# Router logits from raw residual rows, the norm factor on the logits, experts chosen for three tiles then two, rows scaled on GpSimd

## Chip, cores and metric

The kernel runs on 1 core of one Trainium2 chip. The metric is the device time of one execution in microseconds (us). Before the change it is 1668.53 us, the median of 3 runs (1665.18 to 1670.41).

## What is computed

One inference step of a one-layer encoder, over 512 prompt rows and 128 decode rows of width 1024, all in float32. The change is confined to the mixture of experts at the end and to the residual sum ahead of it:

```python
x1 = x + merged @ w_out
y  = x1 + hmoe(x1, ffn_norm_g, ...)

def rmsnorm(x, g):
    return x * lax.rsqrt(jnp.mean(x * x, axis=-1, keepdims=True) + EPS) * g

def mix(hb):                                   # hb: 128 rows of rmsnorm(x1, ffn_norm_g)
    g_logit = hb @ w_group_router + b_group_router            # 4 groups
    g_idx, g_w = argmax(g_logit), softmax(g_logit)[g_idx]
    e_logit = (hb @ w_expert_router + b_expert_router).reshape(-1, 4, 8)[g_idx]
    top_p, top_i = top_k(softmax(e_logit), 2)                 # 2 of the group's 8 experts
    top_p = top_p / sum(top_p)
    combine = one_hot(g_idx * 8 + top_i) * (g_w * top_p)
    hid = silu(hb @ w_exp_gate[e]) * (hb @ w_exp_up[e])       # per expert e, width 256
    return sum over e of (hid * combine[e]) @ w_exp_down[e]
```

## The kernel before

There are five tiles of 128 rows (NT = 5): tiles 0 to 3 are the prompt, tile 4 the decode rows. D_MODEL is cut into KD = 8 pieces of 128. Every engine has its own instruction list, written out by hand in build(), and semaphores hold them together. A float32 matmul of the program shows as two records in the trace.

The end of the program, where the change lies, runs as follows.

1. **Output projection** (TensorE, L1147 to L1160). For each half c of the columns, and in it for each tile t, eight matmuls `merged x w_out` fill a PSUM bank (L1157). The bank of item n is ps[4 + n % 2], so item n waits until VectorE has summed item n-2. VectorE adds each bank to the residual x1 (L2056); the x1 rows were loaded by GpSimd's queue shortly before.
2. **Norm**. After the second half of a tile ScalarE squares and sums x1 (L1612, `h2_squared`), VectorE makes the factor in twelve tiny instructions (`rstd`, L1676 to L1682) and scales the rows into h2 with one instruction (L2015, in `ffn_normed`): x1 times the factor times the gain g_ffn. It reads x1 and the gain with a step of 8 elements, since the expert weights are laid out "(p k)".
3. **Router logits** (TensorE). `h2_transposes(t)` (L1136) makes eight transposes of h2, ScalarE copies them to h2T (L1618), and `router_logits(t)` (L1143) multiplies with the 36 router columns w_rt. Tile t-1 is transposed behind item (t, 1); logits of t-2 stand in the middle of item (t, 1). So tiles 3 and 4 have their transposes or logits behind the last item.
4. **Choice of experts** (VectorE, `route(t0, t1)`, L2018 to L2050). Once for tiles 0 to 3 and once for tile 4, some twenty linked small instructions each. They start only when the last tile is scaled. Their logits lie in ps[2] (tiles 0 to 3) and ps[3].
5. **Ranks** (TensorE, L1170 for tiles 0 to 3; L1174 to L1177 for tile 4 and the totals): how many tokens before this one chose the same expert. `marked_at` (L2080 to L2082, VectorE) turns the ranks into one-hot rows, `pairs_at` (L1183, TensorE) multiplies these with the pair numbers, and `tables` (L2090 to L2093, VectorE) makes the list of rows for each expert.
6. **Experts**. GpSimd gathers the rows of a pair of experts from h2_rows in HBM (L2358, `take_rows`), where it has written the scaled tiles (L2352). TensorE transposes them (L1209), then gate and up (L1223), then down (L1246). Each of 32 experts has 3 MB of weights, in five slots. SyncE's queue refills a slot when the matmuls that read it are done (`gu_full`, `dn_full`): experts 0 to 4 are loaded ahead, expert 5 only after the first gate and up.

```python
for e in range(NES, NE):
    n = (e - NES) // 2
    sp.wait_ge(gu_full, n + 1)
    load_gate(e)
    load_up(e)
    sp.wait_ge(dn_full, 2 * (n + 1))
    load_down(e)
```

The router's weights, biases and the gain are loaded by SyncE's queue (L499 to L503) just before the projection; VectorE waits for all five (rtw_in) before the first bank sum.

## Time and profile before

| | us |
|---|---|
| runs | 1668.53, 1670.41, 1665.18 |
| the profiled execution | 1668.23 |
| its span, first to last instruction | 1666.5 |
| TensorE busy in the span | 1525.9 (92%) |
| VectorE busy | 540.0 (32%) |
| ScalarE busy | 294.9 (18%) |
| GpSimd busy | 112.9 (7%) |
| mean granted TensorE clock | 0.959 |

The profile is one execution. Times in its rows count from the first instruction. Engines are PE (TensorE matmuls), PEld (TensorE weight loads), DVE (VectorE), ACT (ScalarE), POOL (GpSimd) and SP (SyncE); a q behind a name is the engine's sequencer, which issues DMAs. Busy shares are averages over stages with different limits: they don't tell what one stage waits for.

### The profile page before, as it was taken

Reading aid. Unit: us, or ns where it says so; the run is one execution under the profiler, and the core shown is the slowest. Engines: PE = TensorE matmul, PEld = TensorE weight load, DVE = VectorE, ACT = ScalarE, POOL = GpSimd, SP = SyncE. Lnnn points to the kernel's source line nnn. Section 1 sums busy time; section 2 is a strip of 40 time slices with the busy share of each in tenths; the row PEclk is TensorE's granted clock in tenths of the full one; section 3 lists DMA queues with packets and bytes.
Section 4 is the critical chain, followed back from the end, with each engine's and each line's share of the span. In section 5 each row is a group of like instructions: output and inputs, shape, how many; then the busy total and the mean of one; then the engine's idle time right before and its main releaser. Section 6 shows DMA issues by size and latency. Waiting matters only on the chain.

```text
span 1666.5 us, 16956 instructions
## 1 busy us (share of the span) xinstructions
PE 1525.9 (92%) x6626; PEld 848.2 (51%) x6626; DVE 540.0 (32%) x1513; ACT 294.9 (18%) x682; POOL 112.9 (7%) x172
## 2 busy tenths in 40 slices
PE   5999999998799999988999999899999997888882
PEld 3554655445455544455555544566554464444441
DVE  2205498206400031443001144234464263101013
ACT  3214211213200011134110011234300011101010
POOL 6000000112000000000000100100000001101100
PEclk9999999899899999999999999999999978989896
DMA  7331120111331416225112430202014636999985
GB/s 205 114 93 38 39 64 13 51 51 51 115 101 51 151 59 217 78 76 202 51 51 70 157 129 4 64 26 89 26 51 164 283 124 228 420 420 421 421 371 204
DMA packets 127578, 230.88 MB, mean 139 GB/s; under 512 B 12240, under 2 KB 90064, under 8 KB 112528
## 3 DMA queue, kind: packets, MB, share of 16 engines
q1 hardware_dynamic: 114672, 183.03, 30.8%
q0 software_dynamic: 12832, 46.84, 7.9%
q8 instruction: 49, 0.80, 0.2%
q14 instruction: 25, 0.20, 0.0%
HBM read 214.21 MB, written 21.92 MB: 142 GB/s over the span
## 4 chain that ended last, share of the span: by engine, by line
PE 81%; DMA 12%; DVE 4%; ACT 2%; issue 1%; SPq 1%; POOL 0%; POOLq 0%; DVEq 0%; ACTq 0%
PE ps L705 18%; PE ps L724 7%; PE ps L626 7%; PE ps L636 7%; DMA bulk<-in_w_exp_gate 6%; PE ps L1223 5%; PE ps L1157 4%; PE ps L655 3%; PE ps L675 3%; PE ps L585 3%; DMA arena<-in_w_exp_gate 3%; PE ps L627 2%; PE ps L637 2%; PE ps L725 2%; PE ps L747 1%
## 5 line engine op out<-in xcount | busy, mean ns | idle before, releaser
L705 PE MATMUL ps<-bulk 128*128 128x512 f32 x688 | 303.5, 597 | 2.3 <-issue 2.3
L705 PEld LDWEIGHTS ps<-bulk 128*128 128x128 f32 x688 | 129.5, 192 | 156.1 <-issue 156.1
L626 PE MATMUL ps<-bulk 128*128 128x512 f32 x256 | 133.4, 603 | 3.9 <-DMA bulk<-in_w_in 3.9
L1223 PE MATMUL ps<-bulk,arena 128*64 128x256 f32 x736 | 118.2, 422 | 19.8 <-DMA bulk<-in_w_exp_gate 15.0
L724 PE MATMUL ps<-bulk 128*128 128x512 f32 x256 | 135.1, 610 | 0.0
L636 PE MATMUL ps<-arena,bulk 128*128 128x512 f32 x256 | 131.2, 594 | 1.8 <-DVE arena L1792 1.8
L1223 PEld LDWEIGHTS ps<-bulk,arena 128*64 128x64 f32 x736 | 76.5, 153 | 52.0 <-issue 31.8
L627 PEld LDWEIGHTS ps<-bulk 128*128 128x128 f32 x256 | 49.3, 192 | 62.5 <-issue 62.5
L725 PEld LDWEIGHTS ps<-bulk 128*128 128x128 f32 x256 | 48.7, 190 | 61.2 <-issue 61.2
L637 PEld LDWEIGHTS ps<-arena,bulk 128*128 128x128 f32 x256 | 48.7, 190 | 61.2 <-issue 61.2
L1157 PE MATMUL ps<-bulk 128*128 128x512 f32 x160 | 71.8, 606 | 2.1 <-issue 2.1
L1223 PE MATMUL ps<-arena 128*64 128x256 f32 x288 | 60.8, 422 | 11.3 <-DMA arena<-in_w_exp_gate 6.3
L675 PE MATMUL ps<-arena,bulk 128*128 128x512 f32 x128 | 65.6, 594 | 0.8 <-DVE arena L1978 0.8
L585 PE MATMUL ps<-bulk 128*128 128x512 f32 x128 | 65.6, 594 | 0.0
L655 PE MATMUL ps<-bulk 128*128 128x512 f32 x128 | 63.2, 605 | 1.6 <-ACT arena L1385 1.6
L1894 DVE TENSOR_REDUCE st<-mix 128x2 f32<-128x512 f32 (+2 forms) x29 | 18.6, 640 | 131.8 <-ACT mix L1418 131.8
L2155 DVE TENSOR_TENSOR work_all<-mix,ps 128x256 f32<-128x256 f32 x16 | 6.7, 421 | 156.5 <-ACT mix L1640 156.5
L1246 PE MATMUL ps<-bulk,work_all 128*64 128x512 f32 x152 | 47.5, 599 | 6.1 <-ACT work_all L1644 6.1
L1364 ACT ACTIVATE mix<-ps 128x512 f32<-128x512 f32 x16 | 9.6, 597 | 242.0 <-PE ps L627 242.0
L1223 PEld LDWEIGHTS ps<-arena 128*64 128x64 f32 x288 | 36.8, 153 | 25.9 <-issue 20.1
L1157 PEld LDWEIGHTS ps<-bulk 128*128 128x128 f32 x160 | 30.5, 194 | 38.2 <-issue 38.2
L627 PE MATMUL ps<-bulk 128*128 128x128 f32 x256 | 49.7, 276 | 0.0
(397 smaller groups left out, 2057.3 us busy)
## 6 DMA issues: line engine op xcount, KB each, us to landing
bulk<-in_w_exp_up SPq DMA_DIRECT2D x26, 1024.0 KB, 26.2
bulk<-in_w_in SPq DMA_DIRECT2D x48, 512.0 KB, 4.9
bulk<-in_w_exp_gate SPq DMA_DIRECT2D x20, 1024.0 KB, 23.8
bulk<-in_w_exp_down SPq DMA_DIRECT2D x19, 1024.0 KB, 24.8
bulk<-in_w_in SPq DMA_DIRECT2D x7, 2048.0 KB, 10.8
arena<-in_w_exp_down SPq DMA_DIRECT2D x13, 1024.0 KB, 25.3
arena<-in_w_exp_gate SPq DMA_DIRECT2D x12, 1024.0 KB, 25.7
bulk<-in_w_mem_kv SPq DMA_DIRECT2D x4, 2048.0 KB, 9.3
```

Source lines behind the costliest of these rows:

```text
L585: mm(ps[b][:, 0:TP], tw[s][:, k, :], hT[:, k, 0:TP], start=k == 0, stop=k == KD - 1)
L626: mm(ps[4 * q + 1][:, 0:TP], tw[2 * q][:, k, :], hT[:, k, 0:TP], start=k == 0, stop=k == KD - 1)
L627: last = mm(ps[4 * q + 3][:, 0:TS], tw[2 * q][:, k, :], hT[:, k, TP:T], start=k == 0, stop=k == KD - 1)
L636: mm(ps[4 * q][:, 0:TP], tw[2 * q + 1][:, k, :], src[:, k, 0:TP], start=k == 0, stop=k == KD - 1)
L637: last = mm(ps[4 * q + 2][:, 0:TS], tw[2 * q + 1][:, k, :], src[:, k, TP:T], start=k == 0, stop=k == KD - 1)
L655: mm(bank[:, 0:TP], tw[s][:, k, :], hT[:, k, 0:TP], start=k == 0, stop=k == KD - 1)
L675: mm(ps[4 * q][:, 0:TP], tw[s][:, k, :], qaT[:, k, 0:TP], start=k == 0, stop=k == KD - 1)
L705: last = mm(ps[4 + n % 2][:, :], lhs[:, k, tok:tok + P], ring[f % 2][:, k, :], start=k == 0, stop=k == KD - 1)
L724: mm(ps[b][:, 0:TP], tw[s][:, k, :], hT[:, k, 0:TP], start=k == 0, stop=k == KD - 1)
L725: last = mm(ps[b + 1][:, 0:TS], tw[s][:, k, :], hT[:, k, TP:T], start=k == 0, stop=k == KD - 1)
L1157: last = mm(ps[4 + n % 2][:, :], merged[:, k, t * P:(t + 1) * P], ring[f % 2][:, k, :], start=k == 0, stop=k == KD - 1)
L1223: last = mm(ps[2 + s][r, c:c + DF], hsT[s][:, k, r], w[(2 * n + j) % NES][:, k * DF:(k + 1) * DF], start=k == 0, stop=k == KD - 1)
```

## The change

The logits are now made from the raw rows x1: x1 is transposed as soon as it is summed, and the gain is multiplied once into the router's weights (a new small DMA brings it as one value per partition and chunk, gcol_f; the weights' layout becomes "(k p)" for it). The factor of a row is multiplied onto its 36 logits at the head of `route`. `ffn_normed` becomes `ffn_factor`, without the scaling; GpSimd scales the rows in two instructions per tile before it writes them to h2_rows. The choice of experts is cut as tiles 0 to 2 (TA = 3) and tiles 3 and 4. The first `route` stands between the sum of tile 3's last bank and its factor, the marking of tiles 0 to 2 between the last sum and the last factor. On ScalarE the copies of a tile's transposes (now x1T) follow its own square. The ranks of tiles 3 and 4 and the totals are now twice as many matmuls, and wait for the second `route`.

```diff
@@ -208,13 +208,15 @@
 
         x1 = cut(arena, 0, NT * D).rearrange("p (t d) -> p t d", t=NT)
         h2 = [cut(arena, 20 + 4 * n, D) for n in range(2)]
-        h2T = [cut(arena, 28 + 4 * n, KD * P).rearrange("p (k t) -> p k t", k=KD) for n in range(2)]
+        x1T = [cut(arena, 28 + 4 * n, KD * P).rearrange("p (k t) -> p k t", k=KD) for n in range(2)]
         h2_sq = cut(arena, 36, D)
         NR = NG + NE
-        assert D + (KD + 1) * NR <= sum(work_w)
+        assert D + (KD + 1) * NR + KD <= sum(work_w)
+        TA = NT - 2
         g_ffn = work_all[:, 0:D]
         w_rt = work_all[:, D:D + KD * NR].rearrange("p (k c) -> p k c", k=KD)
         b_rt = work_all[:, D + KD * NR:D + (KD + 1) * NR]
+        gcol_f = work_all[:, D + (KD + 1) * NR:D + (KD + 1) * NR + KD]
         rti = sb("rti", 104, I32)
         rt = mix[:, 0:2048]
         rt3 = [rt[:, n * NT * NE:(n + 1) * NT * NE].rearrange("p (t e) -> p t e", t=NT) for n in range(8)]
...
@@ -497,8 +499,10 @@
             for s in range(4):
                 sp.wait_ge(t_full[s], U_MERGE[2] + 4)
             sp.dma_start(g_ffn, a["ffn_norm_g"].partition_broadcast(P)).then_inc(rtw_in, 16)
-            sp.dma_start(w_rt[:, :, 0:NG], a["w_group_router"][0].rearrange("(p k) g -> p k g", p=P)).then_inc(rtw_in, 16)
-            sp.dma_start(w_rt[:, :, NG:NR], a["w_expert_router"][0].rearrange("(p k) g -> p k g", p=P)).then_inc(rtw_in, 16)
+            sp.dma_start(w_rt[:, :, 0:NG], a["w_group_router"][0].rearrange("(k p) g -> p k g", p=P)).then_inc(rtw_in, 16)
+            sp.dma_start(w_rt[:, :, NG:NR], a["w_expert_router"][0].rearrange("(k p) g -> p k g", p=P)).then_inc(rtw_in, 16)
+            with nc.allow_non_contiguous_dma(reason="one gain per partition and chunk"):
+                sp.dma_start(gcol_f, a["ffn_norm_g"][0].rearrange("(k p) -> p k", p=P)).then_inc(rtw_in, 16)
             sp.dma_start(b_rt[:, 0:NG], a["b_group_router"].partition_broadcast(P)).then_inc(rtw_in, 16)
             sp.dma_start(b_rt[:, NG:NR], a["b_expert_router"].partition_broadcast(P)).then_inc(rtw_in, 16)
 
...
-                        last = tr(ps[n % 2][:, k * P:(k + 1) * P], h2[t % 2][:, (4 * h + k) * P:(4 * h + k + 1) * P], ident)
-                    last.then_inc(h2T_full, 1)
+                        last = tr(ps[n % 2][:, k * P:(k + 1) * P], x1[:, t, (4 * h + k) * P:(4 * h + k + 1) * P], ident)
+                    last.then_inc(x1T_full, 1)
 
             def router_logits(t):
 
-                pe.wait_ge(h2T_ok, 2 * (t + 1))
+                pe.wait_ge(x1T_ok, 2 * (t + 1))
                 for k in range(KD):
-                    last = mm(lt_bank(t), h2T[t % 2][:, k, :], w_rt[:, k, :], start=k == 0, stop=k == KD - 1)
-                if t >= NT - 2:
+                    last = mm(lt_bank(t), x1T[t % 2][:, k, :], w_rt[:, k, :], start=k == 0, stop=k == KD - 1)
+                if t in (TA - 1, NT - 1):
                     last.then_inc(rt_full, 1)
 
             for n in index["out"]:
@@ -1150,31 +1154,23 @@
                     pe.wait_ge(ring_in[f % 2], 16 * (f // 2 + 1))
                 pe.wait_ge(*item_out(n - 2))
                 for k in range(KD):
-                    if c and k == KD // 2 and t >= 2:
-                        if t == 2:
-                            pe.wait_ge(rtw_in, 5 * 16)
-                        router_logits(t - 2)
+                    if c and t and k == 2:
+                        x1_transposes(t - 1)
+                    if c and t and k == 6:
+                        if t == 1:
+                            pe.wait_ge(rt_step, 1)
+                        router_logits(t - 1)
                     last = mm(ps[4 + n % 2][:, :], merged[:, k, t * P:(t + 1) * P], ring[f % 2][:, k, :],
                               start=k == 0, stop=k == KD - 1)
                 last.then_inc(n_full, 1)
-                if c and t:
-                    h2_transposes(t - 1)
-            router_logits(NT - 2)
-            h2_transposes(NT - 1)
+
+            pe.wait_ge(rt_step, 2)
+            for t in range(TA):
+                for s in range(t + 1):
+                    last = mm(ps[6][:, t * NE:(t + 1) * NE], before if s == t else ones, hot_both[:, s, :], start=s == 0, stop=s == t)
+            last.then_inc(rank_full, 1)
+            x1_transposes(NT - 1)
             router_logits(NT - 1)
-
-            rank = ps[6]
-            pe.wait_ge(rt_step, 1)
-            for t in range(NT - 1):
-                for s in range(t + 1):
-                    last = mm(rank[:, t * NE:(t + 1) * NE], before if s == t else ones, hot_both[:, s, :], start=s == 0, stop=s == t)
-            last.then_inc(rank_full, 1)
-            pe.wait_ge(rt_step, 2)
-            t = NT - 1
-            mm(ps[4][:, 0:NE], ones, hot_sum, start=True, stop=False)
-            mm(ps[4][:, 0:NE], before, hot_both[:, t, :], start=False, stop=True)
-            mm(ps[4][:, NE:2 * NE], ones, hot_sum, start=True, stop=False)
-            mm(ps[4][:, NE:2 * NE], ones, hot_both[:, t, :], start=False, stop=True).then_inc(rank_full, 1)
 
             def pairs_at(t):
 
@@ -1186,10 +1182,19 @@
                 return last
 
             pe.wait_ge(row_ok, 1)
-            for t in range(NT - 1):
+            for t in range(TA):
                 pairs_at(t)
+            pe.wait_ge(rt_step, 3)
+            for t in range(TA, NT + 1):
+                at_t = ps[4][:, (t - TA) * NE:(t - TA + 1) * NE]
+                mm(at_t, ones, hot_sum, start=True, stop=False)
+                for s in range(TA, min(t + 1, NT)):
+                    last = mm(at_t, before if s == t else ones, hot_both[:, s, :], start=False, stop=s == min(t, NT - 1))
+            last.then_inc(rank_full, 1)
             pe.wait_ge(row_ok, 2)
-            pairs_at(NT - 1).then_inc(take_full, 1)
+            for t in range(TA, NT):
+                last = pairs_at(t)
+            last.then_inc(take_full, 1)
 
             def pairs_over():
 
...
@@ -2005,15 +2008,11 @@
             dve.wait_ge(xr_in, 48)
             gmax, gsum, gw, gidx, m1, m2, dm, e2, i1, i2, den, rden, w0, w1 = rs5[0:14]
 
-            def ffn_normed(t):
+            def ffn_factor(t):
 
                 dve.wait_ge(ssf_ok, t + 1)
                 rstd(rsf[:, t:t + 1], ssf[:, t:t + 1], D)
-                if t >= 2:
-                    dve.wait_ge(h2T_full, 2 * (t - 1))
-                    dve.wait_ge(rows_out[t % 2], ROWS_OUT[t % 2] + 16 * (t // 2))
-                v.scalar_tensor_tensor(h2[t % 2].rearrange("q (k p) -> q k p", k=KD), x1[:, t, :].rearrange("q (p k) -> q k p", k=KD),
-                                       rsf[:, t:t + 1], g_ffn.rearrange("q (p k) -> q k p", k=KD), ALU.mult, ALU.mult).then_inc(h2_ok, 1)
+                dve.sem_inc(h2_ok, 1)
 
             def route(t0, t1):
 
@@ -2030,8 +2029,9 @@
                     link(v.tensor_reduce(out[:, t0:t1], c, AX_X, ALU.min))
 
                 l, e, h0, h1 = lt[:, t0:t1, :], elm[:, t0:t1, :], hot0[:, t0:t1, :], hot1[:, t0:t1, :]
-                src = ps[2][:, 0:nt * NR] if t0 == 0 else ps[3][:, 0:NR]
-                link(v.tensor_tensor(l, src.rearrange("p (t c) -> p t c", t=nt), b_rt.unsqueeze(1).to_broadcast([P, nt, NR]), ALU.add))
+                src = ps[2 if t0 == 0 else 3][:, 0:nt * NR]
+                link(v.tensor_tensor(l, src.rearrange("p (t c) -> p t c", t=nt), per(rsf, NR), ALU.mult))
+                link(v.tensor_tensor(l, l, b_rt.unsqueeze(1).to_broadcast([P, nt, NR]), ALU.add))
                 link(v.tensor_reduce(gmax[:, t0:t1], l[:, :, 0:NG], AX_X, ALU.max))
                 first_index(gidx, l[:, :, 0:NG], gmax, NG)
                 link(v.tensor_tensor(r_tmp[:, t0:t1, :], iota_g[:, t0:t1, :], per(gidx, NE), ALU.not_equal))
@@ -2049,28 +2049,12 @@
                     last = v.tensor_reduce(hot_sum, hot_both[:, 0:nt, :].rearrange("p t e -> p e t"), AX_X, ALU.add)
                 last.then_inc(rt_step, 1)
 
-            dve.wait_ge(rtw_in, 80)
-            for n in index["out"]:
-                _, f, t, c = items[n]
-                dve.wait_ge(n_full, n + 1)
-                v.tensor_tensor(x1[:, t, c * BANK:(c + 1) * BANK], ps[4 + n % 2][:, :], x1[:, t, c * BANK:(c + 1) * BANK], ALU.add)\
-                    .then_inc(x1_ok, 1)
-                if c:
-                    ffn_normed(t)
-
-            dve.wait_ge(rt_full, 1)
-            dve.wait_ge(pool_step, 1 + N_TABLES)
-            route(0, NT - 1)
-            dve.wait_ge(rt_full, 2)
-            route(NT - 1, NT)
-
-
             def per(x, w):
-                return x.unsqueeze(2).to_broadcast([P, NT, w])
+                return x.unsqueeze(2).to_broadcast([P, x.shape[1], w])
 
             def rank_of(t0, t1):
 
-                src = ps[6][:, 0:t1 * NE] if t0 == 0 else ps[4][:, 0:NE]
+                src = ps[6 if t0 == 0 else 4][:, 0:(t1 - t0) * NE]
                 return src.rearrange("p (t e) -> p t e", e=NE)
 
             def marked_at(t0, t1):
@@ -2092,12 +2076,33 @@
                 link(v.tensor_copy(put[0:w, c0:c1], t))
                 return v.tensor_scalar(take[0:w, c0:c1], put[0:w, c0:c1], 1, None, ALU.logical_shift_right)
 
-            for j, hot in enumerate((hot0, hot1)):
-                v.tensor_tensor(at_exp[:, j, :, :], hot, per(pair_id[:, j, :], NE), ALU.mult)
-            dve.wait_ge(rank_full, 1)
-            marked_at(0, NT - 1)
+            def experts_at(t0, t1):
+
+                for j, hot in enumerate((hot0, hot1)):
+                    v.tensor_tensor(at_exp[:, j, t0:t1, :], hot[:, t0:t1, :], per(pair_id[:, j, t0:t1], NE), ALU.mult)
+
+            dve.wait_ge(rtw_in, 16 * 6)
+            v.tensor_tensor(w_rt, w_rt, gcol_f.unsqueeze(2).to_broadcast([P, KD, NR]), ALU.mult).then_inc(rt_step, 1)
+            for n in index["out"]:
+                _, f, t, c = items[n]
+                dve.wait_ge(n_full, n + 1)
+                v.tensor_tensor(x1[:, t, c * BANK:(c + 1) * BANK], ps[4 + n % 2][:, :], x1[:, t, c * BANK:(c + 1) * BANK], ALU.add)\
+                    .then_inc(x1_ok, 1)
+                if c and t == TA:
+                    dve.wait_ge(rt_full, 1)
+                    dve.wait_ge(pool_step, 1 + N_TABLES)
+                    route(0, TA)
+                if c and t == NT - 1:
+                    experts_at(0, TA)
+                    dve.wait_ge(rank_full, 1)
+                    marked_at(0, TA)
+                if c:
+                    ffn_factor(t)
+            dve.wait_ge(rt_full, 2)
+            route(TA, NT)
+            experts_at(TA, NT)
             dve.wait_ge(rank_full, 2)
-            marked_at(NT - 1, NT)
+            marked_at(TA, NT)
             link(v.tensor_tensor(gs5, lt[:, :, 0:NG], per(gmax, NG), ALU.subtract))
             dve.sem_inc(rt_step, 1)
             link(v.tensor_tensor(dm, m2, m1, ALU.subtract))
...
@@ -2349,6 +2354,16 @@
 
             for t in range(NT):
                 pool.wait_ge(h2_ok, t + 1)
+                if t == 0:
+                    pool.wait_ge(rtw_in, 16 * 6)
+                if t >= 2:
+                    pool.wait_ge(rows_out[t % 2], ROWS_OUT[t % 2] + 16 * (t // 2))
+                g.tensor_scalar(h2[t % 2].rearrange("q (k p) -> q k p", k=KD), x1[:, t, :].rearrange("q (p k) -> q k p", k=KD),
+                                rsf[:, t:t + 1], None, ALU.mult).then_inc(pool_step, 1)
+                pool.wait_ge(pool_step, 1 + N_TABLES + 2 * t + 1)
+                g.tensor_tensor(h2[t % 2].rearrange("q (k p) -> q k p", k=KD), h2[t % 2].rearrange("q (k p) -> q k p", k=KD),
+                                g_ffn.rearrange("q (p k) -> q k p", k=KD), ALU.mult).then_inc(pool_step, 1)
+                pool.wait_ge(pool_step, 1 + N_TABLES + 2 * t + 2)
                 g.dma_start(h2_rows[t * P:(t + 1) * P, :], h2[t % 2]).then_inc(rows_out[t % 2], 16)
 
             def at(table, n, w):
```

On TensorE, around the last items of the projection (before: L1157 projection, L1136 transposes, L1143 logits, L1170 to L1177 ranks, L1183 pairs):

```order
L1143 MATMUL ps<-work_all,arena 128x36 x8
L1157 MATMUL ps<-bulk 128x512 x4
L1136 MATMUL ps<-cst,arena 128x128 x8
L1143 MATMUL ps<-work_all,arena 128x36 x8
L1136 MATMUL ps<-cst,arena 128x128 x8
L1143 MATMUL ps<-work_all,arena 128x36 x8
L1170 MATMUL ps<-mix,cst 128x32 x10
L1174 MATMUL ps<-rs,cst 128x32
L1175 MATMUL ps<-mix,cst 128x32
L1176 MATMUL ps<-rs,cst 128x32
L1177 MATMUL ps<-mix,cst 128x32
L1183 MATMUL ps<-wga,wsm 64x16 x20
```

The same place now (L1163 projection, L1140 transposes, L1147 logits, L1170, L1190 and L1192 ranks, L1179 pairs):

```order
L1147 MATMUL ps<-work_all,arena 128x36 x8
L1163 MATMUL ps<-bulk 128x512 x2
L1170 MATMUL ps<-mix,cst 128x32 x6
L1140 MATMUL ps<-cst,arena 128x128 x8
L1147 MATMUL ps<-work_all,arena 128x36 x8
L1179 MATMUL ps<-wga,wsm 64x16 x12
L1190 MATMUL ps<-rs,cst 128x32
L1192 MATMUL ps<-mix,cst 128x32
L1190 MATMUL ps<-rs,cst 128x32
L1192 MATMUL ps<-mix,cst 128x32 x2
L1179 MATMUL ps<-wga,wsm 64x16 x8
```

Tile 3's transposes and logits moved ahead of the last projection matmuls (the last x2 row is the end of the last item); three tiles' ranks and pairs moved ahead of the last routing, and eight rank matmuls stand behind it where four stood.

On VectorE, from the end of the last tile's factor on (before: L2015 scaling, L2034 to L2049 `route`):

```order
L1682 SCALAR_TENSOR_TENSOR st<-st 128x1
L2015 SCALAR_TENSOR_TENSOR arena<-arena,st,work_all 128x1024
L2034 TENSOR_TENSOR mix<-ps,work_all 128x144
L2035 TENSOR_REDUCE rs<-mix 128x4
L2028 TENSOR_TENSOR mix<-mix,rs 128x4x4
```

Now, from the last bank sum (L2089) to the beginning of the last factor (L2082 pair ids, L2064 to L2066 marking of three tiles):

```order
L2089 TENSOR_TENSOR arena<-ps,arena 128x512
L2082 TENSOR_TENSOR wga<-mix 128x96 x2
L2064 TENSOR_TENSOR mix<-mix,ps 128x96
L2065 TENSOR_REDUCE rs<-mix 128x3
L2066 TENSOR_TENSOR wsm<-mix,rs 128x192
L2064 TENSOR_TENSOR mix<-mix,ps 128x96
L2065 TENSOR_REDUCE rs<-mix 128x3
L2066 TENSOR_TENSOR wsm<-mix,rs 128x192
L1679 TENSOR_SCALAR st<-st 128x1
```

The scaling is gone, and the marking of three tiles stands between the last sum and the last factor.

On GpSimd, for each of the five tiles, where only the DMA stood before:

```order
L2361 TENSOR_SCALAR arena<-arena,st 128x1024
L2364 TENSOR_TENSOR arena<-arena,work_all 128x1024
L2367 DMA h_rows<-arena 128x1024
```

The two multiplies are new; each waits for the one before it.

## Rows read from the trace of the kernel before

**Rows 1.** Table of stretches, expert stage (busy time by engine, granted clock, DMA share, GB/s).

```profile
1560.00:1600.00 40.00, 33.42 (x224) 20.78 (x222) 3.61 (x6) 3.49 (x8) 3.02 (x3) 0.88 1.02 421
```

**Rows 2.** Chain of waits, first gather and expert stage (start us, us, what).

```profile
1377.25 4.29 DMA arena<-h_rows,rti
...
1384.24 9.20 PE ps L1223 x64
...
1432.41 22.16 DMA bulk<-in_w_exp_gate
```

**Rows 3.** Timeline of VectorE, bank sums (start, us, what, [idle before <- releaser]).

```profile
1318.35 0.69 DVE L2056 TENSOR_TENSOR arena<-ps,arena 128x512 f32<-128x512 f32 x1 [6.17 <-PE ps L1157]
1325.22 0.69 DVE L2056 TENSOR_TENSOR arena<-ps,arena 128x512 f32<-128x512 f32 x1 [0.57 <-PE ps L1157]
...
1344.28 0.69 DVE L2056 TENSOR_TENSOR arena<-ps,arena 128x512 f32<-128x512 f32 x1 [3.24 <-PE ps L1157]
...
1353.81 0.69 DVE L2056 TENSOR_TENSOR arena<-ps,arena 128x512 f32<-128x512 f32 x1 [3.23 <-PE ps L1157]
```

**Rows 4.** Timeline of VectorE from the last factor to the tables.

```profile
1355.71 0.15 DVE L1676 TENSOR_SCALAR st<-st 128x1 f32<-128x1 f32 x1 [1.21 <-ACT arena L1612]
...
1358.02 2.08 DVE L2015 SCALAR_TENSOR_TENSOR arena<-arena,st,work_all 128x1024 f32<-128x1024 f32 x1
1360.02 0.30 DVE L2034 TENSOR_TENSOR mix<-ps,work_all 128x144 f32<-128x144 f32 x1
...
1366.47 0.20 DVE L2034 TENSOR_TENSOR mix<-ps,work_all 128x36 f32<-128x36 f32 x1 [0.38 <-PE ps L1143]
...
1370.50 0.55 DVE L2096 TENSOR_TENSOR wga<-mix 128x160 f32<-128x160 f32 x2
1370.97 0.28 DVE L2080 TENSOR_TENSOR mix<-mix,ps 128x128 f32<-128x128 f32 x1
...
1372.93 0.18 DVE L2080 TENSOR_TENSOR mix<-mix,ps 128x32 f32<-128x32 f32 x1
...
1374.09 0.17 DVE L2101 TENSOR_TENSOR rs<-mix,rs 128x20 f32<-128x20 f32 x1
...
1375.44 0.23 DVE L2090 TENSOR_SCALAR mix<-ps,mix 128x16 f32<-128x16 f32 x1 [0.85 <-PE ps L1183]
```

**Rows 5.** Timeline of TensorE, ranks and pairs.

```profile
1366.24 4.46 PE L1170 MATMUL ps<-mix,cst 128*128 128x32 f32 x20
...
1373.07 2.32 PE L1183 MATMUL ps<-wga,wsm 128*64 128x16 f32 x40 [0.51 <-DVE wsm L2082]
```

**Rows 6.** Groups of GpSimd's instructions, shapes apart (busy us, mean ns | idle before).

```profile
L2268 POOL COPY arena<-bulk 128x256 f32<-128x256 f32 x2 | 0.7, 386 | 0.8 <-DVE bulk L1802 0.8
```

**Rows 7.** Timelines of GpSimd and VectorE where both work at once.

```profile
358.66 1.26 POOL L2262 TENSOR_TENSOR bulk<-arena,bulk 128x512 f32<-128x512 f32 x1 [20.79 <-ACT bulk L1472]
358.70 1.26 DVE L1801 COPY st<-bulk 128x32 f32<-128x32 f32 x1 [51.28 <-ACT bulk L1472]
...
11.65 0.29 POOL L2205 TENSOR_SCALAR_AFFINE_SELECT cst<-cst 128x128 f32<-128x128 f32 x1
11.73 0.23 DVE L1681 TENSOR_TENSOR st<-st 128x2 f32<-128x2 f32 x1
...
12.18 1.28 DVE L1708 SCALAR_TENSOR_TENSOR arena<-arena,st 128x1024 f32<-128x1024 f32 x1
12.28 1.34 POOL L2205 TENSOR_SCALAR_AFFINE_SELECT cst<-cst 128x128 f32<-128x128 f32 x1
...
375.63 0.68 DVE L1806 TENSOR_TENSOR bulk<-ps,bulk 128x512 f32<-128x512 f32 x1
```

**Rows 8.** Timelines of SyncE's queue and VectorE, router weights and first sums.

```profile
1275.02 7.23 SPq L502 DMA_DIRECT2D work_all<-in_b_group_router  x1
...
1287.18 0.69 DVE L2056 TENSOR_TENSOR arena<-ps,arena 128x512 f32<-128x512 f32 x1 [12.22 <-DMA work_all<-in_b_expert_router]
1290.88 0.69 DVE L2056 TENSOR_TENSOR arena<-ps,arena 128x512 f32<-128x512 f32 x1 [3.01 <-PE ps L1157]
```

38 lines of the change are left out of this document (18 added, 20 removed).

## Prediction

> **What bounds the kernel now.** I read first the table of stretches, then the chain of waits, then the timelines of the stretch between the output projection and the experts. The table shows the expert stage: in a 40 us piece of it the DMA engines are busy the whole time (share 1.02, 421 GB/s) while TensorE is busy for 33.4 us [rows 1]. The stage is bound by the loading of expert weights. The chain says where it is tied to what comes before: the first gather of token rows, then the first gate and up matmuls, then, from 1432.41 on, waits for w_exp_gate [rows 2]. The load queue waits for those first matmuls before it refills a slot, so whatever moves the first gather moves the end by the same amount.
>
> Ahead of the gather stands a serial stretch. In the second half of the projection the bank sums follow each other at 6.87 us where TensorE does only the projection, and at 9.53 us where one tile's transposes and router logits lie between [rows 3]. I count from the start of the last sum, 1353.81, as zero. From there VectorE is busy nearly throughout: norm factor from 1.90 to 4.21, scaling of tile 4, routing of four tiles from 6.21 and of the last from 12.66 to 16.69, marking, and the pair matmuls; the tables that the gather needs start at 1375.44, that is at 21.63 [rows 4]. The ranks of the first four tiles (20 records, 4.46 us) run on TensorE under the routing of the last [rows 5].
>
> **The change, part by part.**
>
> *Later zero.* Tile 3's transposes and logits now stand ahead of the last projection matmuls instead of behind them. Three of the four last gaps were 9.53 us; now all four are: 9.53 - 6.87 = **+2.66 us** [rows 3]. TensorE finds the inputs ready: the sum a transpose needs is done 0.69 us after its bank is full, and two projection steps lie between.
>
> *Routing of three tiles under the projection.* Four tiles took 6.07 us (1360.02 to 1366.47, less 0.38 idle), one took 4.03; so 0.68 per tile, of which I take 0.11 off for the last sum that only the first call makes: 0.57 [rows 4]. Three tiles with one more multiply (0.3) take 5.8. Behind the sum (0.69) and ahead of the norm factor of tile 3 (2.31) that is 8.8 us in a gap of 9.53: it fits, and costs nothing. VectorE is free 0.65 before zero. If it slipped, the last sum would slip with it.
>
> *After zero, without GpSimd.* Sum to 0.69; pair ids of three tiles 0.55, to 1.25; ranks of tiles 0 to 2 are done by then (12 records); marking three tiles: four took 1.96, one 1.16, so 1.7, to 3.0; norm factor 2.31, to 5.3; routing of two tiles 4.03 + 0.57 + 0.26 for the multiply, to 10.2. The scaling by VectorE (2.08) is gone from here. Now a wait is added: the ranks of tiles 3 and 4 and the totals take 16 records, at 0.223 each (4.46/20) 3.6 us, and nothing hides them, where the last ranks used to run under the marking: to 13.8. Marking two tiles 1.43, pairs 16 records at 0.058 (2.32/40) plus 0.1: tables at 16.2 [rows 4, 5]. Against 21.63 that is -5.4, and with the later zero **-2.7 us**.
>
> *Scaling on GpSimd.* Each tile now gets a multiply by the factor (reading x1 with a step of 8 elements) and a multiply by the gain (reading g_ffn with that step). No row shows these. The copy of 256 columns took 0.386, four of them 1.54; the two-input multiply of 512 columns took 1.26, two of them 2.53 [rows 6, 7]. A step of 8 cost VectorE 2.08 instead of 1.28 at 1024 columns [rows 4, 7], 0.80 more. Bounds: 1.54 to 2.34 and 2.53 to 3.33. I take 2.0 and 3.0, the middle and a little, since each reads one strided operand. By themselves the 5.0 us are hidden: tile spacing is 9.53, and the last rows leave GpSimd 10 us ahead of the gather.
>
> They aren't hidden from VectorE. The rows show the two engines shutting each other out for whole instructions: a 32-column copy on VectorE took 1.26, just as long as GpSimd's multiply that began 0.04 earlier; a GpSimd select that takes 0.29 took 1.34 beside a 1.28 VectorE instruction with two inputs in SBUF; a tiny VectorE multiply of two SBUF inputs, begun inside a GpSimd select, ended 0.02 behind it (11.96 against 11.94). A multiply with one input in PSUM ran its 0.68 undisturbed [rows 7]. So instructions with two SBUF inputs wait, those with one don't. The page "SBUF — State Buffer", section "Who interferes with whom", of the Trainium skill says the same: the shared port pair is an exclusive lock, and a VectorE instruction with two SBUF inputs fully blocks behind a GpSimd instruction that reads.
>
> Where do they meet? Tiles 0 to 2: GpSimd works from about 4.3 to 9.4 after the tile's sum, while VectorE has nothing to do. Tile 3: GpSimd starts at -0.6. Its first multiply holds until 1.4, so the first pair-id instruction waits 0.7; the second multiply slips in behind it, 1.7 to 4.7, and the second pair-id instruction waits. Marking ends at 6.65 instead of 3.0, the factor of tile 4 at 9.0. Tile 4: GpSimd starts at 9.05, exactly with the last routing. That waits from 9.3 to 11.05 (bias add), and from 11.5 to 14.3 (first comparison): 4.55 lost. Routing ends at 9.0 + 4.86 + 4.55 = 18.4; ranks 22.0; marking 23.45; tables 24.5. Against 21.63 that is +2.85, with the zero's 2.66 **+5.5 us**.
>
> *Router weights.* One more small DMA (1024 elements of 4 bytes), then a 0.3 us multiply, stand ahead of the first sum. That sum waits for these weights already, and its bank is needed again only when the next one's matmuls are done: 1290.88 - 1287.18 - 0.69 = 3.0 us of cover [rows 8]. The queue spent 7.23 us in one issue there [rows 8]; another one would cost 7.2 + 0.3 - 3.0 = 4.5, none would cost 0. I take 0: the next bias load took its turn at once behind it. The ScalarE copies and squares stay; nothing of them is waited for longer.
>
> Sum: the profiled execution took 1668.23 (span 1666.5), + 5.5 = 1673.7. The median shown is 0.3 higher, so I forecast **1674.0**.
>
> **Rivals.**
>
> *No shutting out.* If GpSimd takes only gaps, or VectorE's short two-input instructions get through, the 8.2 us go and the change gives -2.7: 1665.8, not slower. It decides from the point where less than 2.8 of the 8.2 us are really waited. For it: the select that began at 11.65 delayed a VectorE instruction by less than the 0.23 that it took. Against it: the copy that stood for 1.26.
>
> *Strided reads cost GpSimd half as much again.* 1.54 and 2.53 become 2.3 and 3.8; both tiles' waits grow by 0.3 + 0.8, so +2.2: 1676.2. For it: VectorE pays 62% for the same step. Against it: GpSimd takes 2.5 ns a column in the two-input multiply, which may cover a slower read. The Trainium skill, page "GPSIMD Engine Reference", section "Performance pitfalls for Q7 kernels", has such a rule: a read step above 8 bytes costs 50% more per element. No run here shows it yet.
>
> *Router weights late.* The stall above, half of 4.5 on the forecast: 1676.3. Against it: 3.0 us of cover.
>
> *The change doesn't do what it says.* If the routing of three tiles doesn't fit into the gap, the last sum slips by what is missing; above 0.65 that adds to the forecast one for one, within its range.
>
> **How the numbers follow.** A measurement of this kernel can tell about 0.3% (5.0 us) from no change: slower means above 1673.5. Forecast 0.50, its own range 1671 to 1677, and somewhat more than half of it above the bound: 0.30 slower, 0.20 same. No shutting out 0.22: 0.19 same, 0.03 faster. Strided reads 0.18: 0.17 slower, 0.01 same. Weights late 0.10: 0.09 slower, 0.01 faster for an unseen gain. Together slower 0.56, same 0.40, faster 0.04. Even the best case lies 2.3 us short of faster, so the sign hangs on GpSimd. The range takes in most of the first rival at 1665.8 and the two slower ones: 1666.0 to 1678.5.
>
> **What would show it.** Right: sums at 9.53 us up to the last; VectorE instructions of the last routing that take over 1 us, ending with a GpSimd instruction; ranks of 16 records with VectorE idle for some 3 us; GpSimd at 2.0 and 3.0 per tile; the tables 24.5 after the last sum; the expert stage as long as before. Wrong: short instructions all through the last routing, tables at 16 to 18 (first rival); a first bank sum that holds up TensorE (third); an expert stage of another length, which no step here expects.

## The result: 0.4% slower, and the profile after

The changed kernel takes 1674.62 us (median of 10 runs, 1672.54 to 1678.31) against 1668.94 for the kernel before, run beside it: a ratio of 1.0037, with a 95% interval of 1.0026 to 1.0048. A second pass of the same kernel, later on (e9 below), gave 1.0027 (1.0016 to 1.0038). The profiled execution took 1675.58, with a span of 1673.4 and a mean granted clock of 0.957 (before: 0.959).

The stage of the experts is bound by the loading of weights as before. The table of stretches of the changed kernel, with the columns of [rows 1], has the same DMA share and the same rate; here the stretch between projection and experts stands with it:

```profile
1360.00:1386.00 26.00, 10.76 (x93) 10.10 (x91) 19.96 (x59) 2.55 (x6) 14.72 (x7) 0.58 0.41 162
1560.00:1600.00 40.00, 31.79 (x194) 17.16 (x190) 4.94 (x8) 3.49 (x8) 4.04 (x4) 0.87 1.02 421
```

In the first line GpSimd is busy for 14.72 of 26 us: that is new. The chain of waits goes the way of [rows 2], from the gather through the first gate and up matmuls to the waits for w_exp_gate:

```profile
1385.69 4.20 DMA arena<-h_rows,rti
...
1392.59 9.94 PE ps L1228 x64
...
1441.48 21.91 DMA bulk<-in_w_exp_gate
```

So the gather's start decides here too. It comes 1385.69 - 1377.25 = 8.4 us later than before, but the span ends only 1673.4 - 1666.5 = 6.9 us later: from the gather to the end it is 287.7 us, where it was 289.3. In the other profiles of this study that stretch takes 286.7 to 288.8 us. Why the one profile of the kernel before has the longest is not shown.

The bank sums, VectorE's timeline, answer to [rows 3]:

```profile
1321.93 0.69 DVE L2089 TENSOR_TENSOR arena<-ps,arena 128x512 f32<-128x512 f32 x1 [6.17 <-PE ps L1163]
1331.46 0.69 DVE L2089 TENSOR_TENSOR arena<-ps,arena 128x512 f32<-128x512 f32 x1 [5.34 <-PE ps L1163]
...
1350.52 0.69 DVE L2089 TENSOR_TENSOR arena<-ps,arena 128x512 f32<-128x512 f32 x1 [5.34 <-PE ps L1163]
...
1360.04 0.69 DVE L2089 TENSOR_TENSOR arena<-ps,arena 128x512 f32<-128x512 f32 x1 [0.42 <-PE ps L1163]
```

From tile 0's on, all four gaps are 9.53 us now; one of them was 6.87. In the last gap VectorE still waits 0.42 us for the bank: the routing of three tiles and the factor of tile 3 fit into it.

From the last sum to the tables, the same timeline, answering to [rows 4]. The long small instructions are what to look for:

```profile
1360.65 1.56 DVE L2082 TENSOR_TENSOR wga<-mix 128x96 f32<-128x96 f32 x2
1362.14 0.24 DVE L2064 TENSOR_TENSOR mix<-mix,ps 128x96 f32<-128x96 f32 x1
...
1364.38 2.25 DVE L1683 SCALAR_TENSOR_TENSOR st<-st 128x1 f32<-128x1 f32 x1
1366.67 0.16 DVE L1684 TENSOR_TENSOR st<-st 128x1 f32<-128x1 f32 x1
...
1368.33 0.23 DVE L2033 TENSOR_TENSOR mix<-ps,st 128x72 f32<-128x72 f32 x1
1368.60 1.92 DVE L2034 TENSOR_TENSOR mix<-mix,work_all 128x72 f32<-128x72 f32 x1
...
1370.95 0.17 DVE L2028 SCALAR_TENSOR_TENSOR mix<-mix 128x8 f32<-128x8 f32 x1
...
1372.38 2.80 DVE L2028 SCALAR_TENSOR_TENSOR mix<-mix 128x64 f32<-128x64 f32 x1
...
1381.21 0.22 DVE L2064 TENSOR_TENSOR mix<-mix,ps 128x64 f32<-128x64 f32 x1 [3.44 <-PE ps L1192]
...
1383.87 0.23 DVE L2074 TENSOR_SCALAR mix<-ps,mix 128x16 f32<-128x16 f32 x1 [0.74 <-PE ps L1179]
```

And GpSimd beside it; no row of the trace before showed these multiplies:

```profile
1359.79 3.88 POOL L2361 TENSOR_SCALAR arena<-arena,st 128x1024 f32<-128x1024 f32 x1 [6.75 <-DVEq L2015]
1363.75 2.86 POOL L2364 TENSOR_TENSOR arena<-arena,work_all 128x1024 f32<-128x1024 f32 x1
1366.91 0.61 POOL L2367 DMA_DIRECT2D h_rows<-arena  x1 [0.30 <-POOL arena L2364]
1368.35 3.81 POOL L2361 TENSOR_SCALAR arena<-arena,st 128x1024 f32<-128x1024 f32 x1 [0.83 <-DVEq L2015]
1372.25 2.84 POOL L2364 TENSOR_TENSOR arena<-arena,work_all 128x1024 f32<-128x1024 f32 x1
```

One element per partition (L1683) takes 0.16 us undisturbed, here 2.25, and ends at 1366.63; GpSimd's second multiply ends at 1366.61. L2028 takes 2.80 and ends at 1375.18, GpSimd's at 1375.09. So a VectorE instruction with two inputs in SBUF waits there until GpSimd's two-input multiply is over. The four long ones (L2082, L1683, L2034, L2028) lost 1.14, 2.10, 1.69 and 2.57 us against their like nearby, for the pair of L2082 the 0.42 that it takes in e1 below; 7.5 together. L2033 and the last sum (L2089), with one input in PSUM, run at their normal length beside GpSimd's first multiply. From about 2.2 us into that multiply on, instructions with two inputs in SBUF do too: L2066 takes 0.36 us at 1362.70, and L2028 0.17 at 1370.95.

TensorE, answering to [rows 5]: the ranks of the last two tiles now stand alone, in six pieces of 16 records, after 10.68 us in which TensorE waited for VectorE, and only 16 records of the pairs are left behind them:

```profile
1377.55 0.64 PE L1190 MATMUL ps<-rs,cst 128*128 128x32 f32 x2 [10.68 <-DVE mix L2046]
...
1380.13 1.04 PE L1192 MATMUL ps<-mix,cst 128*128 128x32 f32 x4
1382.78 1.04 PE L1179 MATMUL ps<-wga,wsm 128*64 128x16 f32 x16 [1.61 <-DVE wsm L2066]
```

The tables start 1383.87 - 1360.04 = 23.83 us after the last sum, 2.20 more than the 21.63 before. With the 2.66 by which the last sum is later within the projection, the steps of the change make +4.9 us of the 5.7 between the medians. The rest of the profiled difference lies ahead of the change: VectorE and TensorE come to the projection 3.6 us later. These are the first projection matmuls, of the kernel before, of the changed one, and of the changed one in e9:

```profile
1275.18 6.23 PE L1157 MATMUL ps<-bulk 128*128 128x512 f32 x10 [2.06 <-issue]
```

```profile
1278.76 2.81 PE L1163 MATMUL ps<-bulk 128*128 128x512 f32 x3 [2.06 <-issue]
```

```profile
1277.92 3.65 PE L1163 MATMUL ps<-bulk 128*128 128x512 f32 x4 [2.06 <-issue]
```

One program, two executions, 0.8 us apart. The variants below, which share all the code up to there, come between 1275.8 (e5) and 1278.8 (e6), so executions alone differ by up to 3 us there. In this pair 2.9 of the 3.6 us are there already at TensorE's wait for w_in, at 448 us, which took 3.87 us before and 6.00 in the changed kernel's execution; but e1 waits 6.51 us at that place and still comes to the projection at 1276.4. I therefore compare two distances inside a profile, which don't depend on the arrival: the gaps between the sums, and the tables from the last sum.

### The profile page after: what moved, and what is told of

It is laid out like the page before. It is cut to its first block, busy times and chain, and to the rows that moved or that the text cites. A ratio compares the mean times of both kernels' runs of the same rounds, so it can differ in the third digit from the quotient of the medians.

```text
span 1673.4 us, 16972 instructions
## 1 busy us (share of the span) xinstructions
PE 1523.2 (91%) x6626; PEld 843.8 (50%) x6626; DVE 538.6 (32%) x1513; ACT 295.4 (18%) x682; POOL 146.6 (9%) x182
## 4 chain that ended last, share of the span: by engine, by line
PE 80%; DMA 12%; DVE 4%; ACT 2%; issue 1%; SPq 1%; POOL 0%; POOLq 0%; DVEq 0%; ACTq 0%
PE ps L709 18%; PE ps L728 7%; PE ps L630 7%; PE ps L640 7%; DMA bulk<-in_w_exp_gate 6%; PE ps L1228 5%; PE ps L1163 4%; PE ps L659 3%; PE ps L679 3%; PE ps L589 3%; DMA arena<-in_w_exp_gate 3%; PE ps L631 2%; PE ps L641 2%; PE ps L729 2%; PE ps L751 1%
## 5 line engine op out<-in xcount | busy, mean ns | idle before, releaser
L709 PEld LDWEIGHTS ps<-bulk 128*128 128x128 f32 x688 | 129.3, 191 | 155.9 <-issue 155.9
L631 PEld LDWEIGHTS ps<-bulk 128*128 128x128 f32 x256 | 49.2, 192 | 62.5 <-issue 62.5
L729 PEld LDWEIGHTS ps<-bulk 128*128 128x128 f32 x256 | 48.6, 190 | 61.2 <-issue 61.2
L1163 PE MATMUL ps<-bulk 128*128 128x512 f32 x160 | 72.2, 606 | 2.1 <-issue 2.1
L641 PE MATMUL ps<-arena,bulk 128*128 128x128 f32 x256 | 49.2, 274 | 0.0
```

The lines of the kernel that those rows point to most:

```text
L631: last = mm(ps[4 * q + 3][:, 0:TS], tw[2 * q][:, k, :], hT[:, k, TP:T], start=k == 0, stop=k == KD - 1)
L641: last = mm(ps[4 * q + 2][:, 0:TS], tw[2 * q + 1][:, k, :], src[:, k, TP:T], start=k == 0, stop=k == KD - 1)
L709: last = mm(ps[4 + n % 2][:, :], lhs[:, k, tok:tok + P], ring[f % 2][:, k, :], start=k == 0, stop=k == KD - 1)
L729: last = mm(ps[b + 1][:, 0:TS], tw[s][:, k, :], hT[:, k, TP:T], start=k == 0, stop=k == KD - 1)
L1163: last = mm(ps[4 + n % 2][:, :], merged[:, k, t * P:(t + 1) * P], ring[f % 2][:, k, :], start=k == 0, stop=k == KD - 1)
```

## The experiments

Two theories stood against each other. **Shutting out**: GpSimd's multiplies make VectorE's two-input instructions wait, and without that the change would be a gain. **No shutting out**: the long instructions have another cause. Beside these I tested each further term of the sum. The first four kernels ran on one chip, the next four on one, the last three on one, each beside the kernel before.

**e1: no scaling at all.** GpSimd writes the rows from x1.

```diff
-                g.tensor_scalar(h2[t % 2].rearrange("q (k p) -> q k p", k=KD), x1[:, t, :].rearrange("q (p k) -> q k p", k=KD),
-                                rsf[:, t:t + 1], None, ALU.mult).then_inc(pool_step, 1)
-                pool.wait_ge(pool_step, 1 + N_TABLES + 2 * t + 1)
-                g.tensor_tensor(h2[t % 2].rearrange("q (k p) -> q k p", k=KD), h2[t % 2].rearrange("q (k p) -> q k p", k=KD),
-                                g_ffn.rearrange("q (p k) -> q k p", k=KD), ALU.mult).then_inc(pool_step, 1)
-                pool.wait_ge(pool_step, 1 + N_TABLES + 2 * t + 2)
-                g.dma_start(h2_rows[t * P:(t + 1) * P, :], h2[t % 2]).then_inc(rows_out[t % 2], 16)
+                g.dma_start(h2_rows[t * P:(t + 1) * P, :], x1[:, t, :]).then_inc(rows_out[t % 2], 16)
```

> GpSimd's two multiplies are left out: the rows for the experts are written from x1 as it stands, unscaled, so that part of the computation is missing. Everything else is the changed kernel. Theory (GpSimd's multiplies shut VectorE out): after the last bank sum the changed kernel lost 1.14 + 2.10 + 1.69 + 2.57 = 7.5 us in four VectorE instructions that ended with a GpSimd multiply or inside one. Here none takes over 0.4 us, the tables of the gather start at about 23.8 - 7.5 = 16.3 us after the last sum (forecast 16.2), and the time is 7 to 8 us under the changed kernel, 1667. Rival (the long instructions have another cause, GpSimd's work only lies beside it): tables stay near 23.8 and the time within 1 us of the changed kernel. Rival (something behind the tables takes the gain back, for instance the expert weights' queue): tables at 16.3 and a time near 1674.

Measured: 1666.58 us, 0.9986 of the kernel before (0.9973 to 0.9998). The last sum and the tables in VectorE's timeline:

```profile
1355.96 0.69 DVE L2089 TENSOR_TENSOR arena<-ps,arena 128x512 f32<-128x512 f32 x1 [1.00 <-PE ps L1163]
1356.56 0.42 DVE L2082 TENSOR_TENSOR wga<-mix 128x96 f32<-128x96 f32 x2
1357.21 0.26 DVE L2064 TENSOR_TENSOR mix<-mix,ps 128x96 f32<-128x96 f32 x1 [0.23 <-PE ps L1170]
...
1369.95 0.22 DVE L2064 TENSOR_TENSOR mix<-mix,ps 128x64 f32<-128x64 f32 x1 [3.44 <-PE ps L1192]
...
1372.61 0.23 DVE L2074 TENSOR_SCALAR mix<-ps,mix 128x16 f32<-128x16 f32 x1 [0.75 <-PE ps L1179]
```

The tables come 16.66 after the sum; the two pair-id instructions take 0.42 together instead of 1.56. So GpSimd's multiplies cost 23.83 - 16.66 = 7.2 us of the stretch. The median lies 1.9 us under that of the kernel before beside it, where the changed kernel lay 5.7 and, in its second pass, 4.5 above: 7.6 and 6.4 us apart. The wait of 3.44 for the ranks is the same to the digit. Shutting out holds, the two rivals fall.

**e2: VectorE scales in place**, each tile right behind its factor, with the instruction of before; GpSimd only writes.

```diff
                 rstd(rsf[:, t:t + 1], ssf[:, t:t + 1], D)
-                dve.sem_inc(h2_ok, 1)
+            def scaled(t):
+                if t >= 2:
+                    dve.wait_ge(rows_out[t % 2], ROWS_OUT[t % 2] + 16 * (t // 2))
+                v.scalar_tensor_tensor(h2[t % 2].rearrange("q (k p) -> q k p", k=KD), x1[:, t, :].rearrange("q (p k) -> q k p", k=KD),
+                                       rsf[:, t:t + 1], g_ffn.rearrange("q (p k) -> q k p", k=KD), ALU.mult, ALU.mult).then_inc(h2_ok, 1)
...
                 if c:
                     ffn_factor(t)
+                    scaled(t)
```

> VectorE scales each tile right behind its factor, in one instruction as before the change (2.08 us); GpSimd only writes rows. Routing stays as in the changed kernel. Theory: four of the five scalings have room; that of tile 3 stands ahead of the last sum, where VectorE was free about 0.4 us before, so the last sum slips by 2.08 - 0.4 = 1.7, and that of tile 4 puts 2.08 into the stretch behind it, the shutting out (7.5) goes: 1.7 + 2.08 - 7.5 = -3.7 against the changed kernel, about 1671. Rival (no shutting out): +3.8, 1678.

Measured: 1668.98 us, 0.9999 (0.9982 to 1.0016). The last gap between sums grew to 10.56, so the last sum slipped by 1.03, not 1.7: without GpSimd VectorE has 1.00 us of room there (e1), not 0.4. The tables come 18.24 after it, 0.5 less than e1's 16.66 with one scaling of 2.1 added. The 2.1 us instruction on VectorE costs less than the 6.7 us on GpSimd that took its place. Both distances together are 4.6 us shorter than in the changed kernel, where I expected 3.7.

**e3: VectorE scales late**: tiles 0 to 2 as in e2, tiles 3 and 4 behind the last routing.

```diff
+                if c and t < TA:
+                    scaled(t)
...
             experts_at(TA, NT)
+            for t in range(TA, NT):
+                scaled(t)
             dve.wait_ge(rank_full, 2)
```

> VectorE scales tiles 0 to 2 right behind their factors, tiles 3 and 4 behind the last routing, while TensorE makes the ranks (VectorE waited 3.44 us for them in the changed kernel). Two scalings take 4.16, of which 0.7 stick out. Theory: -7.5 + 0.7 = -6.8 against the changed kernel, about 1668, that is 1 us under the kernel before; tables at 17.0 after the last sum. Rival (no shutting out): +0.7 on the changed kernel. Rival (the rows of tile 4 land too late for the gather): the gather waits for the write, not for the tables.

Measured: 1666.60 us, 0.9990 (0.9978 to 1.0001). Tables 17.17 after the last sum:

```profile
1357.86 0.69 DVE L2095 TENSOR_TENSOR arena<-ps,arena 128x512 f32<-128x512 f32 x1 [1.07 <-PE ps L1163]
...
1368.29 4.17 DVE L2020 SCALAR_TENSOR_TENSOR arena<-arena,st,work_all 128x1024 f32<-128x1024 f32 x2
```

Of 4.17 us of scaling, 17.17 - 16.66 = 0.5 show. The wait for the ranks is a place for work that the change leaves empty.

**e4: GpSimd reads with a step of one**, same multiplies.

```diff
-                g.tensor_scalar(h2[t % 2].rearrange("q (k p) -> q k p", k=KD), x1[:, t, :].rearrange("q (p k) -> q k p", k=KD),
-                                rsf[:, t:t + 1], None, ALU.mult).then_inc(pool_step, 1)
+                g.tensor_scalar(h2[t % 2], x1[:, t, :], rsf[:, t:t + 1], None, ALU.mult).then_inc(pool_step, 1)
...
-                g.tensor_tensor(h2[t % 2].rearrange("q (k p) -> q k p", k=KD), h2[t % 2].rearrange("q (k p) -> q k p", k=KD),
-                                g_ffn.rearrange("q (p k) -> q k p", k=KD), ALU.mult).then_inc(pool_step, 1)
+                g.tensor_tensor(h2[t % 2], h2[t % 2], g_ffn, ALU.mult).then_inc(pool_step, 1)
```

> GpSimd multiplies the same 1024 columns twice, but reads x1 and the gain with a step of one element instead of eight (the elements of a row then stand in another order than the reference wants; the amount of work is the same). If the step is what made the first multiply take 3.85 us: it takes 1.9 or less here and the second 2.5. If a multiply by a per-partition factor is that slow on GpSimd whatever the step: 3.8 again. Shutting out: VectorE's long instruction behind the first multiply took 2.2 of its 3.85 us; if the lock is tied to the reading, it shrinks with the multiply; the time is then up to 2 us under the changed kernel.

Measured: 1670.18 us (one run). GpSimd's timeline, then VectorE's:

```profile
1356.33 2.84 POOL L2361 TENSOR_SCALAR arena<-arena,st 128x1024 f32<-128x1024 f32 x1 [7.70 <-DVEq L2015]
1359.26 2.34 POOL L2363 TENSOR_TENSOR arena<-arena,work_all 128x1024 f32<-128x1024 f32 x1
...
1364.16 2.84 POOL L2361 TENSOR_SCALAR arena<-arena,st 128x1024 f32<-128x1024 f32 x1 [1.66 <-DVEq L2015]
```

```profile
1357.16 0.69 DVE L2089 TENSOR_TENSOR arena<-ps,arena 128x512 f32<-128x512 f32 x1 [1.00 <-PE ps L1163]
1357.77 0.42 DVE L2082 TENSOR_TENSOR wga<-mix 128x96 f32<-128x96 f32 x2
...
1359.84 1.97 DVE L2066 TENSOR_TENSOR wsm<-mix,rs 128x192 f32<-128x192 f32 x1
...
1364.41 0.94 DVE L2034 TENSOR_TENSOR mix<-mix,work_all 128x72 f32<-128x72 f32 x1
...
1378.20 0.23 DVE L2074 TENSOR_SCALAR mix<-ps,mix 128x16 f32<-128x16 f32 x1 [0.75 <-PE ps L1179]
```

Neither expectation holds as put: the first multiply takes 2.84, not 1.9 and not 3.8. The step costs it 1.0 us (35%) and the second multiply 0.5 us (22%); the larger part of the first one's length is the instruction itself. And its lock is shorter than it is. The pair ids at 1357.77 began 1.44 us into a multiply of 2.84 and were not held at all; L2034 began 0.25 into the next one and was let go 1.19 after that one's start. With the step of eight, in the changed kernel, L2034 was let go 2.17 after the start of a multiply of 3.81 (2.17 in e5 and e9 too). Both values of the hold, which take in the 0.23 us of L2034 itself, differ by the 1.0 us by which the multiplies differ, so about 1.65 us at the end of each hold nothing. The value for the step of one rests on one instruction. The two-input multiply holds to its end (L2066 ends at 1361.81, GpSimd at 1361.60). The tables come 21.04 after the last sum, 2.8 sooner than in the changed kernel: so much of the loss is the step's. The remaining holds, 1.61, 0.71 and 2.06 us (the last in a second L2028), add up to the 4.4 by which 21.04 lies above e1's 16.66.

**e5: the totals behind the signal.** Six of the 16 records for which VectorE waits are needed only later.

```diff
-                at_t = ps[4][:, (t - TA) * NE:(t - TA + 1) * NE]
+                at_t = ps[4][:, (t - TA) * NE:(t - TA + 1) * NE] if t < NT else ps[6][:, TA * NE:(TA + 1) * NE]
...
-            last.then_inc(rank_full, 1)
+                if t == NT - 1:
+                    last.then_inc(rank_full, 1)
```

> The changed kernel with one edit: the six matmul records of the totals come behind the signal for which VectorE waits, and into another bank; they are needed only behind the tables. If the ranks of tiles 3 and 4 are exposed (VectorE waited 3.44 us for 16 records, 0.215 each), ten records leave 2.15: tables at 23.83 - 1.3 = 22.5 us after the last sum, and 1.3 us less, about 1673. Rival (the wait is the way from VectorE to TensorE and back, whatever the number of records): no change.

Measured: 1671.69 us, 1.0022 (1.0009 to 1.0035). VectorE waits 2.16 instead of 3.44, and the tables come 22.53 after the last sum, 1.30 sooner, as expected:

```profile
1376.93 0.22 DVE L2065 TENSOR_TENSOR mix<-mix,ps 128x64 f32<-128x64 f32 x1 [2.16 <-PE ps L1192]
```

**e6: GpSimd only where VectorE rests.** GpSimd scales tiles 0 to 2, VectorE tiles 3 and 4 as in e3.

```diff
                 rstd(rsf[:, t:t + 1], ssf[:, t:t + 1], D)
-                dve.sem_inc(h2_ok, 1)
+                if t < TA:
+                    dve.sem_inc(h2_ok, 1)
...
+            for t in range(TA, NT):
+                scaled(t)
             dve.wait_ge(rank_full, 2)
...
                 pool.wait_ge(h2_ok, t + 1)
+                if t < TA:
...
```

> GpSimd scales tiles 0 to 2, as in the changed kernel, and VectorE tiles 3 and 4 behind the last routing, as in e3. If GpSimd's multiplies cost only where VectorE has two-input work beside them: the first three lie where VectorE waits, but the end of tile 2's second multiply holds the first routing by some 0.6 us, for which there is 0.4 to 1.0 us of room ahead of the last sum. So within 0.5 us of e3: tables at about 17.2 after the last sum, 1667. Rival (GpSimd's work costs in itself, through its DMA or its order): up to 3/5 of the changed kernel's loss, +4 us on e3.

Measured: 1667.52 us, 0.9986 (0.9970 to 1.0001), against 0.9990 for e3; the tables come 17.22 after the last sum (e3: 17.17), with 0.51 us of room ahead of it (e3: 1.07). GpSimd's three scalings cost nothing there. What costs is the overlap, and it is all in tiles 3 and 4.

**e7: the logits of tile 3 behind the projection**, built on e3 and e5.

```diff
                     if c and t and k == 6:
...
-                        router_logits(t - 1)
+                        if t < NT - 1:
+                            router_logits(t - 1)
...
             x1_transposes(NT - 1)
+            router_logits(NT - 2)
             router_logits(NT - 1)
...
-                rstd(rsf[:, t:t + 1], ssf[:, t:t + 1], D)
+                t0 = TA if t >= TA else t
+                rstd(rsf[:, t0:t + 1], ssf[:, t0:t + 1], D)
...
-                if c:
+                if c and t != TA:
                     ffn_factor(t)
```

> e3 with the router logits of tile 3 moved from between the last projection matmuls to behind the transposes of tile 4, where TensorE waits for ScalarE's copies; one norm factor instruction chain for tiles 3 and 4 together; the totals as in e5. The logits of a tile take (9.53 - 6.87) / 2, about 1.3 us, of the gap: the last sum comes 1.3 us sooner (a last spacing of 8.2), the tables stay at 17.2 after it, if the logits of both tiles are ready when the factor is: 1.3 us under e3, about 1665.3. Rival: the logits of tile 4 come later by the same 1.3 and the second routing waits for them: no gain.

Measured: 1665.35 us, 0.9977 (0.9967 to 0.9987); once more in e10. The last gap is 7.74, 1.8 less than 9.53 where I expected 1.3: of the 2.66 us that transposes and logits take together, the logits are the larger part and not half (in the changed kernel the last projection matmuls follow 1.70 us behind the start of the logits, and 0.87 behind that of the transposes). And the tables come 17.56 after the sum, 0.4 later than in e3: 0.44 us of that is a wait of the second routing for the logits. The profile's first and last sum of the gap:

```profile
1349.40 0.69 DVE L2100 TENSOR_TENSOR arena<-ps,arena 128x512 f32<-128x512 f32 x1 [3.23 <-PE ps L1164]
1357.14 0.69 DVE L2100 TENSOR_TENSOR arena<-ps,arena 128x512 f32<-128x512 f32 x1 [1.38 <-PE ps L1164]
```

**e8: one marking for five tiles**, behind the second routing, with a scaling on either side of it. On TensorE the ranks of tiles 0 to 2 go behind the second logits, and the totals into another bank.

```diff
                     experts_at(0, TA)
-                    dve.wait_ge(rank_full, 1)
-                    marked_at(0, TA)
...
-            for t in range(TA, NT):
-                scaled(t)
-            dve.wait_ge(rank_full, 2)
-            marked_at(TA, NT)
+            scaled(TA)
+            dve.wait_ge(rank_full, 1)
+            marked_at(0, NT)
+            scaled(NT - 1)
```

> e7, and the marking of tiles 0 to 2 goes behind the second routing, together with that of tiles 3 and 4; VectorE scales tile 3 while TensorE makes the ranks and tile 4 while it does the 40 records of the pairs. By durations of the trace: sum 0.7, pair ids to 1.25, factor from 1.9 to 4.2, routing to 9.2, pair ids to 9.5, scaling of tile 3 to 11.6 (ranks done at 11.4), marking of five tiles (four took 1.96) to 13.9, pairs 40 x 0.058 + 0.1 beside the scaling of tile 4: tables at 16.4 against 17.2: 0.8 us under e7, about 1664.5. Rival: the logits of tile 4 aren't ready at 4.2, and the second routing waits: no gain over e7. Rival: the rows of tile 4 land behind the tables, and the gather waits for them: the gain is lost.

Measured: 1666.28 us, 0.9981 (0.9970 to 0.9993): no gain over e7, as far as the two intervals can tell. Both rivals came true. The second routing starts 5.44 after the last sum, having waited 1.19 for the logits, and GpSimd's timeline shows the gather waiting for a DMA, not for the tables:

```profile
1375.07 0.53 POOL L2366 DMA_DIRECT2D h_rows<-arena  x1 [3.96 <-DVE arena L2021]
1378.81 1.10 POOL L2372 DMA_INDIRECT arena<-h_rows,rti  x1 [3.20 <-DMA h_rows<-arena]
```

The tables started at 1375.35; in e7 the gather follows them by 1.80, here by 3.46. From the end of a scaling to the gather of its rows is 4 us (1374.78 to 1378.81), so the last scaling must end by 2.2 us ahead of the tables.

**e9 and e10: the changed kernel and e7 again, side by side.**

> The changed kernel itself, once more. Its steps account for 2.66 + 2.20 = 4.9 us over the kernel before; its profiled execution also came 3.6 us late to the output projection, in code that the change doesn't touch, where the variants came between 0.5 us early and 3 us late. If that is a difference between executions, the first pass here is at another time and the ratio stays near 1.003. If it belongs to the changed program, the same 3.6 us show again.

> e7 once more, beside the changed kernel on the same chip: 0.997 to 0.999 of the kernel before, and 8 to 9 us under the changed kernel.

Measured: 1674.14 us, 1.0027 (1.0016 to 1.0038), with the tables 23.79 after the last sum; and 1664.60 us, 0.9974 (0.9962 to 0.9986), with 17.56: 9.5 us apart, where I expected 8 to 9. The first projection matmul of e9 came at 1277.92, neither at 1278.76 nor at 1275.18. So it wasn't at the place of the first time, and e5, which differs from the changed kernel only behind the projection, came at 1275.77. All twelve profiles after the change lie 0.6 to 3.6 us behind the one trace of the kernel before, 2.4 in the mean; with one trace of before, how much of it is the changed program's stays open. The medians ask for none of it: the table below accounts for them without it.

**e11: ScalarE shares the scaling.** ScalarE multiplies tiles 3 and 4 by the factor while VectorE routes; VectorE multiplies by the gain, which ScalarE has put into the rows' order once, ahead of the first sum.

```diff
+            act.wait_ge(rtw_in, 16 * 6)
+            go(h2[0].rearrange("q (k p) -> q k p", k=KD), g_ffn.rearrange("q (p k) -> q k p", k=KD), ACT.Copy).then_inc(ssf_ok, 1)
+            act.wait_ge(ssf_ok, 1)
+            go(g_ffn, h2[0], ACT.Copy).then_inc(ssf_ok, 1)
...
+            act.wait_ge(rt_step, 3)
+            for t in range(TA, NT):
+                act.wait_ge(rows_out_in[t % 2], ROWS_OUT[t % 2] + 16 * (t // 2))
+                go(h2[t % 2].rearrange("q (k p) -> q k p", k=KD), x1[:, t, :].rearrange("q (p k) -> q k p", k=KD),
+                   ACT.Copy, scale=rsf[:, t:t + 1]).then_inc(ssf_ok, 1)
...
+                if t >= TA:
+                    dve.wait_ge(ssf_ok, NT + t - TA + 3)
+                    v.tensor_tensor(h2[t % 2], h2[t % 2], g_ffn, ALU.mult).then_inc(h2_ok, 1)
+                    return
```

> e7, but the scaling of tiles 3 and 4 is shared: ScalarE, which waits there for 13 us, multiplies by the norm factor and writes the row in the order wanted (a scaled copy, about 1.1 us a tile by its 1.06 for a square of 1024 columns), and VectorE only multiplies by a gain that lies in the same order, with a step of one (1.28 by the row of such an instruction, instead of 2.1). ScalarE brings the gain into that order once, ahead of the first sum (2 us, beside the projection). VectorE has 1.6 us less behind the routing: tables at 17.6 - 1.6 = 16.0 after the last sum. But the wait for the ranks (10 records, 2.2) must still be hidden, which 2.6 us of multiplies just do. About 1.6 us under e7. Rival: the permuted copies on ScalarE cost far more than 1.1 (a step of eight): up to 8 us for two tiles they still fit between the factor and the end of the routing, above that the gain goes. Rival: ScalarE is itself held by VectorE's work: its copies end late.

Measured: 1662.32 us, 0.9957 (0.9943 to 0.9971): the lowest median of the study, about 7 us under the kernel before and 12 under the changed one (the interval just meets that of e10). Tables 15.68 after the last sum. ScalarE's copies in its timeline, those of tiles 3 and 4 and those of the gain, and VectorE's two multiplies:

```profile
1361.35 4.18 ACT L1641 ACTIVATE arena<-arena,st 128x1024 f32<-128x1024 f32 x2 [2.53 <-DVEq L2031]
```

```profile
1289.88 2.07 ACT L1632 ACTIVATE arena<-work_all 128x1024 f32<-128x1024 f32 x1 [86.74 <-DMA work_all<-in_b_expert_router]
1291.98 1.06 ACT L1634 ACTIVATE work_all<-arena 128x1024 f32<-128x1024 f32 x1
```

```profile
1366.73 2.35 DVE L2037 TENSOR_TENSOR arena<-arena,work_all 128x1024 f32<-128x1024 f32 x2
```

ScalarE's scaled copies take 2.1 us a tile with the step of eight, twice what I expected (the two copies that bring the gain into order, early, show the step's part: 2.07 with it, 1.06 without), and still end 1.2 us ahead of VectorE's first multiply. VectorE's routing beside them runs undisturbed. The gather now starts 1.80 after the tables, with the last rows' landing as its releaser: both end together.

All of it by the two distances: the four gaps from tile 0's last sum to tile 4's, together 35.46 us before, and the tables from the last sum, 21.63 before (in e8 the gather's extra 1.66 is added). The ratio is the difference over 1668.5:

| kernel | gaps | tables | against before | as ratio | measured ratio |
|---|---|---|---|---|---|
| changed | 38.11 | 23.83 | +4.9 | 1.0029 | 1.0037, 1.0027 |
| e1 no scaling | 38.12 | 16.66 | -2.3 | 0.9986 | 0.9986 |
| e2 VectorE in place | 39.15 | 18.24 | +0.3 | 1.0002 | 0.9999 |
| e3 VectorE late | 38.19 | 17.17 | -1.7 | 0.9990 | 0.9990 |
| e4 step of one | 38.11 | 21.04 | +2.1 | 1.0012 | one run |
| e5 totals behind | 38.11 | 22.53 | +3.6 | 1.0021 | 1.0022 |
| e6 GpSimd early | 38.19 | 17.22 | -1.7 | 0.9990 | 0.9986 |
| e7 logits late | 36.33 | 17.56 | -3.2 | 0.9981 | 0.9977, 0.9974 |
| e8 one marking | 36.33 | 17.73 + 1.66 | -1.4 | 0.9992 | 0.9981 |
| e11 ScalarE shares | 36.33 | 15.68 | -5.1 | 0.9970 | 0.9957 |

Every measured interval holds the value from the two distances, that of e11 at its edge. They carry the change. What e8 and e11 gained beyond them, about 2 us each, lies inside their intervals and stays unexplained; their profiles have the shortest stretches from the gather to the end, 286.7 and 286.8 us.

## Why the prediction was right

The forecast was 1674.0, the median 1674.62, and the case that it rested on (GpSimd shuts VectorE out, once per multiply, in tiles 3 and 4) is the one that e1, e3 and e6 show. The two numbers lie closer together than the working: the steps of the change make +4.9 us where the sum had +5.5. The profiled execution also held two differences that no step has, 3.6 us of late arrival and 1.5 us less behind the gather. By its steps:

- **Later zero**, +2.66: the gaps sum to 38.11 instead of 35.46, +2.65.
- **Routing of three tiles under the projection**, at nothing: the first route took 6.3 us (forecast 5.8; 0.6 of it a wait for GpSimd's second multiply of tile 2, which I had not seen coming), and VectorE was free 0.42 ahead of the sum instead of 0.65. It fits, but with less to spare than put.
- **After zero without GpSimd**, tables at 16.2: e1 has 16.66. Of the 0.46, 0.23 is a wait for the ranks of tiles 0 to 2, which I had called done.
- **Exposed ranks**, 16 records, 3.6 us: VectorE waited 3.44, and e5 shows that the number of records sets it (1.30 us for six).
- **GpSimd's multiplies**, 2.0 and 3.0 us: 3.85 and 2.85. The first is the term that was mis-sized, nearly twofold, and above its bound of 2.34. I had bounded it from a plain copy, which has no multiply by a column of factors; e4 shows that even without the step it takes 2.84.
- **Locks**, 8.2 us: 7.5 by the four instructions, 7.2 by e1. The sum is right in part by luck, since two errors cancel: the first multiply is 1.85 us longer than put, but holds only 2.2 us of its 3.85, close to the 2.0 that I had given it as a whole. Had it held to its end, each of the two tiles would have lost about 1.65 us more (an estimate from e4's rows). It also moved the second multiplies later: that of tile 3 hit the norm factor (L1683) instead of the pair ids and the marking.
- **Tables** at 24.5: 23.83. **Router weights** at nothing: VectorE's multiply took 0.46 and the second sum still waited for its bank, with 2.81 us of idle time where the sum before had 3.01 [rows 8]. The new DMA's issue took 2.33 us, and that of the bias behind it fell from 7.23 to 4.99: the queue time only moved. **The expert stage** "as long as before": from the gather to the end it was 1.5 us shorter, 287.7 against 289.3.

```profile
1278.28 2.33 SPq L505 DMA_DIRECT2D work_all<-in_ffn_norm_g  x1
1280.66 4.99 SPq L506 DMA_DIRECT2D work_all<-in_b_group_router  x1
```

```profile
1290.59 0.46 DVE L2085 TENSOR_TENSOR work_all<-work_all 128x288 f32<-128x288 f32 x1 [12.05 <-DMA work_all<-in_b_expert_router]
1290.97 0.68 DVE L2089 TENSOR_TENSOR arena<-ps,arena 128x512 f32<-128x512 f32 x1
1294.46 0.69 DVE L2089 TENSOR_TENSOR arena<-ps,arena 128x512 f32<-128x512 f32 x1 [2.81 <-PE ps L1163]
```

The rivals: *no shutting out* is refuted (e1). *Strided reads* were real, at 35% and 22% instead of half as much again, and they lengthened the waits: by e4 they are 2.8 us of the 23.83 to the tables. They didn't move the time above the forecast, as the rival had it, because the forecast's 2.0 and 3.0 already covered what holds, 2.2 and 2.85. *Router weights late* is refuted: the second sum comes 15.70 us after the first projection matmul, as before. So is *the change doesn't do what it says*: VectorE still waited 0.42 us for the last bank. The Trainium skill, page "GPSIMD Engine Reference", section "Performance pitfalls for Q7 kernels", puts a read step above 8 bytes at 50% more per element. Here the step is 32 bytes; an estimate by that rule makes 4.3 of the 2.84 and 3.5 of the 2.34 (where only one of two inputs has the step), but 3.85 and 2.85 were measured.

The prediction took from the rows of before that instructions shut each other out as wholes. The Trainium skill, page "SBUF — State Buffer", section "Who interferes with whom", also calls the shared port pair an exclusive lock. For GpSimd's two-input multiply the rows after agree (held until 0.02 to 0.2 us past its end). For its multiply by one input and a column they don't: 1.2 us of 2.84, 2.2 us of 3.85. And one sentence of the prediction doesn't fit its own rows: instructions with one SBUF input, it says, don't wait, but the 32-column copy that stood for 1.26 us has only one [rows 7]. Inside GpSimd's second multiply VectorE's one-input L1681 took its normal 0.15 us (at 1364.19); no copy met a multiply after the change, so why that one waited stays open.

## What to carry to other kernels

Before an engine is given work because it is idle, look at what its neighbour does in the same microseconds: three scalings on GpSimd cost nothing in the time where VectorE mostly waited (e6), and two cost 7.2 us where it ran short two-input instructions, more than the same two on VectorE in place (2.6 us by the two distances, e2 against e1). A wait on the critical path is a better place for the work than a second engine: VectorE's own two scalings under the wait for the ranks cost 0.5 of their 4.2 us (e3). ScalarE took half of that work without slowing VectorE's instructions beside it (e11). When an edit shortens one chain, ask when its side product (here the rows that the gather reads) must have landed; e8 lost its gain there.

## What the runs showed of the hardware

- GpSimd's multiply of 128x1024 f32 by a column of factors takes 2.84 us with a read step of one and 3.85 with a step of eight; its multiply of two tiles 2.34, and 2.85 with one of them at that step. The two-input instruction is the faster one.
- A VectorE instruction with two SBUF inputs that meets the first is done 1.2 us (step of one, e4) and 2.2 us (step of eight) after its start, and those that begin later run at their normal length; one that meets the second is done 0.02 to 0.2 us after its end. One with an input in PSUM is held by neither (L2033 at 1368.33, 0.23 us; L2089, 0.69, at 1360.04 beside the first and at 1350.52 beside the second).
- A step of eight on the input costs ScalarE's copy of 1024 columns 1.0 us (2.07 against 1.06, e11) and VectorE's scaling 0.8 (2.08 against the 1.28 of the same instruction without the step [rows 7]).
- With a further small DMA ahead of it on SyncE's queue, the issue of the group bias took 4.9 to 5.4 us instead of 7.23, and the new issue 2.2 to 2.5, in all twelve profiles: the sum stayed within 0.7 us.
